# Attention steps of a two-layer decoder kernel: every pair of heads takes its query blocks from the longest to the shortest

## The reference

```python
def sb_block(q, k, v, bias, q_pos, k_pos):
    z = jnp.einsum('bqhd,bkhd->bhqk', q.astype(F32), k.astype(F32)) * (DH_A ** -0.5)
    z = z + bias.astype(F32)[None, :, None, None]
    mask = k_pos[None, :] < q_pos[:, None]
    lneg = jnp.where(mask, jax.nn.log_sigmoid(-z), 0.0)
    tail = lax.cumsum(lneg, axis=3, reverse=True) - lneg
    a = jnp.where(mask, jnp.exp(jax.nn.log_sigmoid(z) + tail), 0.0)
    return jnp.einsum('bhqk,bkhd->bqhd', a, v.astype(F32))
```

## Time and profile before

| | us |
|---|---|
| runs shown: median (lowest to highest of 3) | 2274.99 (2272.51 to 2287.51) |
| the profiled execution's own time | 2272.9 |
| its span | 2271.1 |
| VectorE's first scan of block 8 in pass 2, pass 4 | 419.72, 515.28 |
| next stage's first matmul | 564.26 |

### The profile page before, as it was taken

How to read it: one execution, slowest core, us unless ns; L and a number is a source line. 1 busy time by engine, 2 the same in 40 slices (tenths; PEclk the granted TensorE clock), 3 DMA queues, 4 the chain that set the end, 5 groups by cost and what they waited for, 6 DMA issues and landing times. The chain is left out here.

```text
span 2271.1 us, 28108 instructions
## 1 busy us (share of the span) xinstructions
PE 2021.5 (89%) x11281; PEld 1619.0 (71%) x11281; DVE 1102.9 (49%) x1799; ACT 658.3 (29%) x1167; POOL 94.6 (4%) x149
## 2 busy tenths in 40 slices
PE   5999988877566989999999799899999999948998
PEld 5999986555332439999999585595586577637885
DVE  5331114887230224543444457755856856765351
ACT  4211113776220113322222322331232232242221
POOL 0000000000000000000000001101100110110000
PEclk9999998999788999999999898997999999979999
DMA  4111114000767204776594325524543534664651
GB/s 150 41 40 56 57 29 147 6 1 7 230 182 223 69 33 80 124 138 150 117 205 138 133 91 182 183 87 158 192 157 116 209 125 139 245 227 135 188 156 33
DMA packets 177128, 282.66 MB, mean 124 GB/s; under 512 B 15236, under 2 KB 110280, under 8 KB 175883
## 3 DMA queue, kind: packets, MB, share of 16 engines
q1 hardware_dynamic: 152597, 191.51, 30.3%
q0 software_dynamic: 24256, 88.82, 10.7%
q10 hardware_dynamic: 144, 0.52, 0.1%
HBM read 185.70 MB, written 95.31 MB: 124 GB/s over the span
## 5 line engine op out<-in xcount | busy, mean ns | idle before, releaser
L1392 PE MATMUL pre_ps<-x_xh,pre_wh 128*128 128x358 f32 (+1 forms) x792 | 261.0, 330 | 6.7 <-DVE pre_wl L1514 6.7
L1393 PE MATMUL pre_ps<-norm_xl,pre_wh 128*128 128x358 f32 (+1 forms) x792 | 259.8, 328 | 0.0
L1394 PE MATMUL pre_ps<-x_xh,pre_wl 128*128 128x358 f32 (+1 forms) x792 | 259.4, 328 | 0.0
L426 PE MATMUL proj_ps<-x_xe,proj_wh 128*128 128x368 f32 x480 | 161.1, 336 | 4.8 <-DVE proj_wl L539 4.8
L428 PE MATMUL proj_ps<-x_xe,proj_wl 128*128 128x368 f32 x480 | 159.5, 332 | 0.0
L427 PE MATMUL proj_ps<-lo_xl,proj_wh 128*128 128x368 f32 x480 | 159.2, 332 | 0.0
L1392 PEld LDWEIGHTS pre_ps<-x_xh,pre_wh 128*128 128x128 f32 x792 | 150.4, 190 | 8.1 <-DVE pre_wl L1514 7.2
L1393 PEld LDWEIGHTS pre_ps<-norm_xl,pre_wh 128*128 128x128 f32 x792 | 150.3, 190 | 0.0
L1394 PEld LDWEIGHTS pre_ps<-x_xh,pre_wl 128*128 128x128 f32 x792 | 150.3, 190 | 0.0
L1820 PE MATMUL head_ps<-head_cl,head_wh 128*128 128x358 f32 (+1 forms) x384 | 125.2, 326 | 0.0
L1819 PE MATMUL head_ps<-head_ch,head_wh 128*128 128x358 f32 (+1 forms) x384 | 125.0, 325 | 0.0
(11 more groups left out here) (404 smaller groups left out, 4088.8 us busy)
## 6 DMA issues: line engine op xcount, KB each, us to landing
head_Cs<-in_state_C POOLq DMA_DIRECT2D x32, 1024.0 KB, 5.8
out_C_s<-head_Cs POOLq DMA_DIRECT2D x32, 1024.0 KB, 4.7
x_xnT<-in_cache_sb_k SPq DMA_DIRECT2D x64, 256.0 KB, 2.9
all_w<-in_w_in_c SPq DMA_DIRECT2D x32, 512.0 KB, 9.4
all_w<-in_w_in_a SPq DMA_DIRECT2D x24, 512.0 KB, 3.9
paged_vp<-in_cache_sb_v SPq DMA_DIRECT2D x48, 256.0 KB, 2.9
x_dram<-low_low SPq DMA_DIRECT2D x16, 536.0 KB, 9.3
ca_dram<-low_low SPq DMA_DIRECT2D x16, 536.0 KB, 10.0
```

The lines of the kernel that those rows point to most:

```text
L426: pe.matmul(out, wh[:, t % 2, k, :], xh[:, k, c0:c1], start=(k == 0), stop=False)
L1392: pe.matmul(out, wh[:, t % 2, k, :], xh[:, k, c0:c1], start=(k == 0), stop=False)
L1393: pe.matmul(out, wh[:, t % 2, k, :], xl[:, k, c0:c1], start=False, stop=False)
L1394: last = pe.matmul(out, wl[:, t % 2, k, :], xh[:, k, c0:c1], start=False, stop=(k == KD - 1))
```

## The change

The list of steps is the only thing that differs: all four pairs now go from block 8 down to block 0. Pairs 1 and 3 are as before, and pairs 0 and 2 are reversed. The steps next to each other where a pair ends are then always block 0 and block 8.

```diff
 def attention_steps(nc, d, const, half, biasB, biasN, biasR, biasR_in, mixT, qT, kT, v, kt_out, v_out, table, kp, k_in, vp0, v_in0):
 
-    GROUPS = [(p, t) for p in range(PAIRS) for t in (range(NT + 1) if p % 2 == 0 else range(NT, -1, -1))]
+    GROUPS = [(p, t) for p in range(PAIRS) for t in range(NT, -1, -1)]
     NG = 2
```

## The result

| | before | with the change |
|---|---|---|
| median of 20 runs, us (lowest to highest) | 2274.59 (2268.92 to 2287.51) | 2287.57 (2275.52 to 2295.2) |
| ratio, 95% interval | | 1.0046 (1.0029 to 1.0063) |
| profiled execution, us; span | 2272.9; 2271.1 | 2295.2; 2293.4 |
| attention stage, first scores to next stage's first matmul | 367.63 to 564.26: 196.63 | 369.06 to 572.50: 203.44 |

The account below looks back on a forecast made before the run. VectorE, busy 159.9 us of the 198.2 us stage, was taken to set the floor. First scan at 374.6, four passes of 42.85, three junctions of 5.13 and a 3.40 tail gave +0.5 us: 2273.4, stated as 2274, range 2266 to 2288.

Parts of the forecast that it names:

- The start: Stage opening: block 8's scores come first, mostly at low clock, 4.2 us, then 2.81 to the first scan.
- Blocks 8, 7 and 6: Downward pass, scan of 8 to scan of 6: 15.4 us in place of 18.13, one score at low clock.
- The refund: Blocks 8 to 6: block 0's tiny copies and transposes precede each pass, so 15.4 us in place of 18.13.
- The junctions: Three joints from block 0 to block 8: VectorE waits almost all of 5.13 us, 7.45 at most.
- The rest of a pass and the tail: Scan of 6 to the pass's end stays 27.45 us; last pass's end to next stage 3.40.
- Rival A: Low clock after every junction slows blocks 8 to 6 and block 5's scores: 12 us more, 2285; chance 0.15.
- B: VectorE-bound throughout: full clock in blocks 8 to 6, 14.56 us per pass, early start: 2269; chance 0.2.
- C: Slower by more than 1%: clock stays low between junctions and TensorE becomes the bound, 2297; chance 0.04.
- D: Faster by more than 1%: needs a stage of 175 us, where at least 183 was reckoned; chance 0.02.

Follow-up runs that it names:

- e4: Changed kernel plus 14 unused bf16 matmuls in TensorE's wait ahead of block 7's scores; ratio 1.0019, stage 199.72 us.
- e5: Changed kernel plus 14 unused matmuls in TensorE's wait ahead of block 7's scores and 14 in its next wait; ratio 0.9973, stage 196.50 us.
- e12: Kernel before plus 10 unused matmuls in TensorE's first wait inside the transposes of each block 8 and 7; ratio 0.9953, stage 188.39 us.
- e6: Kernel before plus 10 unused matmuls in TensorE's first wait inside the transposes of each block 8, 7, 6 and 5; ratio 0.9983, stage 192.02 us.
- e3: Kernel before plus four memsets on VectorE at the end of the attention stage; ratio 1.0044, stage 204.99 us.

## Why the prediction was wrong

The sum of the parts, as measured in the changed kernel, is 6.33 + (17.32 + 16.03 + 17.56 + 17.70) + 4 x 27.43 + 3 x 5.13 + 3.40 = 203.45 us, against 197.2 forecast.

1. *The start.* Forecast 4.2 + 2.81 = 6.97, measured 375.39 - 369.06 = 6.33. Right within its range.
2. *Blocks 8, 7 and 6: the step that failed.* I wrote that one of the two scores would be at low clock, as in before, and took 15.4. Measured 16.0 to 17.7, in three of four passes above the upper bound of 16.9 that I had for both. The change moves block 7's scores behind a wait of 3.18 us and block 6's behind one of 2.6 to 3.0, where TensorE's longest wait from block 8's second scores to block 6's had been 1.47 in before, so what before showed was no guide to it. The upper bound was too low as well: I stretched the two scores and left the copies and transposes between them at 2.83 us, and they too ran at low clock, 3.39. This term is 7.0 us too small over the four passes (68.6 against 61.6); part 1 took 0.6 of that back. e4 and e5 show it directly: where TensorE is kept busy in these waits, passes 2 to 4 take 15.3, which is the number of the forecast with its premise of one score hit. The refund that I counted on, no long copies behind block 8, is whole only at that clock: 2.7 us per pass were counted on, 0.4 to 2.1 came. The order's own cost was in the sum; what the sum lacked was clock.
3. *The junctions.* Forecast 5.13, measured 425.27 - 420.14 = 5.13 and twice 5.12. The moved outputs of block 2 cost nothing, as argued: VectorE's step of block 1 grew from 2.25 to 3.50 us inside that idle time.
4. *The rest of a pass and the tail.* 27.43 and 3.40, forecast 27.45 and 3.40.

Rival A, low clock after every junction, had the mechanism, with 2285 and a chance of 0.15. I had weighed it by the trace of before, in which the 0 to 0 joint keeps full clock. But at that joint TensorE has no long wait. A was to be judged by the new joint's own wait, which I had worked out just before: 4.63 us less two small jobs. The Trainium skill, "TensorE: Matmul & The Clock Gate", section "Why this matters for your kernels", advises against idle gaps between bursts of matmuls, since the clock then falls to half. The new junctions agree with it: a wait of 3.18 us, and 0.50 to 0.57 behind it. The row of before that I named for it does not show it so well, since ahead of 432.9 no wait was longer than 1.47 us.

A's other half, that block 5's scores would be hit too, did not happen: from block 6 on all passes ran as before. So A priced the stage 12 us above the forecast and 6.3 came; that the median of 2287.57 lies so near its 2285 is in part luck. B's full clock in blocks 8 to 6 was seen in no pass of the changed kernel, not even with fillers. C and D did not occur. C was priced on one low stretch per pass in before, outside the start; its trace has five in four passes (from 412.4, 432.9, 484.1, 507.9 and 528.5 us). And the forecast took 1% for what a measurement can tell here, where 20 runs of each kernel gave an interval of 0.17% to either side.

## What to carry to other kernels

When an order is changed, look at where the matmul engine waits in each. A wait of a few us ahead of work on the critical chain can cost twice, once itself and once through the clock of what follows. Price every link of the chain behind such a wait at low clock, the small transposes too, and do not take the clock of a place from a trace in which that place had no wait. Where the wait can't be removed, a few unused matmuls in it can be worth more than the order: here 0.47%, where the reordering lost 0.46%.

## What the runs showed of the hardware

- The clock fell although TensorE was far from idle. Ahead of 432.9 us in before it had been busy for 12.14 of 16.8 us. With ten unused bf16 matmuls of 256 columns (1.25 us of work) in one wait of each step of blocks 8 and 7, it stayed at 1.00 from 379 us to the end of e12's stage. With fillers in blocks 6 and 5 as well (e6) it did not.
- The same instructions meet the low clock at other places in another execution: from 411 to 440 us e3 had 1.00 throughout, where before was at 0.50 at 413 and 433.
- An fp32 matmul with 64 rows of keys overlaps one on the other 64 rows entirely: 0.73 us for the pair at 272 columns, 0.72 for one.
